# A chunked scan's software pipeline: four matrices made in two rounds, output parts in a kept bank, other rounds for most steps

## The reference, cut to what matters

```python
def wkv7_scan(state0, r, w, k, v, a_vec, b_vec, reverse):
    def step(S, inp):
        r_t, w_t, k_t, v_t, a_t, b_t = inp
        sa = jnp.einsum('bhij,bhj->bhi', S, a_t)
        S = (S * w_t[:, :, None, :] + sa[..., None] * b_t[:, :, None, :]
             + v_t[..., None] * k_t[:, :, None, :])
        return S, jnp.einsum('bhij,bhj->bhi', S, r_t)
    s_fin, ys = lax.scan(step, state0, xs, reverse=reverse)
```

## Time and profile before

| what | us |
|---|---|
| runs, median (lowest, highest) | 2563.83 (2563.2, 2566.87) |
| profiled execution, first to last instruction | 2557.6 |
| PE busy in it | 2362.5 |
| stretch of the scan, first to last triangular copy | 1429 to 1748 |

### The profile page before, as it was taken

One profiled execution on the slowest core, in us unless ns is written; L12 is line 12 of the kernel. 1 busy time (PEld: TensorE's weight loads), 2 busy tenths in 40 slices (PEclk: granted clock), 3 DMA queues, 4 the chain that ended last, 5 costly groups with the idle time before them and its releaser, 6 DMA issues.

```text
span 2557.6 us, 38789 instructions
## 1 busy us (share of the span) xinstructions
PE 2362.5 (92%) x15040; PEld 1754.2 (69%) x15040; DVE 1744.3 (68%) x3348; ACT 1052.7 (41%) x2064; POOL 338.9 (13%) x534
## 2 busy tenths in 40 slices
PE   7999999799989799899999899988999998998997
PEld 3788887464888699843454577776577765766775
DVE  4875787677756687723657666666678884748996
ACT  4222222224221434421144244433467783346884
POOL 0111110010001011000200233331012210001210
PEclk9999999899999999999998999999899999999998
DMA  8555654242326488511110000000379993115995
GB/s 302 198 201 193 221 196 157 89 149 80 109 73 216 148 279 277 201 50 58 36 39 33 34 3 3 2 2 2 106 255 352 337 323 112 71 58 204 343 336 203
DMA packets 115064, 386.98 MB, mean 151 GB/s; under 512 B 20161, under 2 KB 22337, under 8 KB 114625
## 3 DMA queue, kind: packets, MB, share of 16 engines
q1 hardware_dynamic: 76640, 276.33, 30.6%
q0 software_dynamic: 34848, 95.47, 10.9%
q10 hardware_dynamic: 3392, 12.70, 1.3%
HBM read 389.66 MB, written 26.21 MB: 163 GB/s over the span
## 4 chain that ended last, share of the span: by engine, by line
PE 36%; DVE 14%; DMA 7%; ACT 5%; issue 3%; POOL 0%; DVEq 0%; ACTq 0%; SPq 0%; POOLq 0%
PE ps L143 34%; DMA RG<-in_w 5%; DVE moe0wl L152 3%; PE ps L146 2%; DVE moe1wl L152 2%; DMA AR<-in_a 2%; DVE rwMM L172 1%; DVE f2wl L152 1%; DVE acc L160 1%; ACT moe0wh L149 1%; DVE H L160 1%; ACT moe1wh L149 1%; DVE rwXF L152 1%; ACT rwWU L149 1%; DVE rwXX L152 0%
## 5 line engine op out<-in xcount | busy, mean ns | idle before, releaser
L143 PE MATMUL ps<-H,RG 128*128 128x256 f32 (+2 forms) x1088 | 360.1, 487 | 14.0 <-ACT H L149 14.0
L160 DVE SCALAR_TENSOR_TENSOR acc<-AR,cs,acc 128x512 f32<-128x512 f32 x420 | 295.4, 746 | 43.3 <-DMA AR<-in_a 41.5
L143 PEld LDWEIGHTS ps<-H,RG 128*128 128x128 f32 (+1 forms) x1088 | 205.3, 192 | 151.3 <-issue 135.0
L152 DVE TENSOR_TENSOR moe0wl<-RG,moe0wh 128x1024 fp32r<-128x1024 f32 x144 | 173.7, 1220 | 39.1 <-ACT moe0wh L149 35.0
L149 ACT ACTIVATE moe0wh<-RG 128x1024 fp32r<-128x1024 f32 x144 | 151.1, 1061 | 69.9 <-DMA RG<-in_w 37.4
L199 POOL DMA_DIRECT2D AR<-in_a x152 | 82.2, 541 | 696.5 <-DVE acc L160 506.2
L149 ACT ACTIVATE f1wh<-RG 128x1024 fp32r<-128x1024 f32 x66 | 69.7, 1061 | 229.9 <-PE ps L143 229.8
L152 DVE TENSOR_TENSOR moe1wl<-RG,moe1wh 128x1024 fp32r<-128x1024 f32 x120 | 144.3, 1219 | 21.3 <-ACT moe1wh L149 17.8
L143 PE MATMUL ps<-f1hh,f1wh 128*128 128x512 f32 x352 | 142.7, 405 | 4.6 <-DVE f1hl L152 4.6
L149 ACT ACTIVATE moe1wh<-RG 128x1024 fp32r<-128x1024 f32 x120 | 126.1, 1060 | 44.0 <-DMA RG<-in_w 24.5
L143 PE MATMUL ps<-f1hh,f1wl 128*128 128x512 f32 x352 | 141.3, 401 | 0.0
(11 more groups left out here) (634 smaller groups left out, 5765.9 us busy)
## 6 DMA issues: line engine op xcount, KB each, us to landing
RG<-in_w SPq DMA_DIRECT2D x525, 512.0 KB, 4.7
AR<-in_a POOLq DMA_DIRECT2D x152, 512.0 KB, 3.7
moe0back<-moe_outs ACTq DMA_DIRECT2D x4, 1024.0 KB, 8.1
CT<-in_consts ACTq DMA_DIRECT2D x1, 2546.0 KB, 13.3
X<-in_x ACTq DMA_DIRECT2D x1, 2048.0 KB, 11.7
moe_rows<-moe0ht POOLq DMA_DIRECT2D x4, 512.0 KB, 4.9
moe1back<-moe_outs ACTq DMA_DIRECT2D x2, 1024.0 KB, 5.9
X<-in_ctx ACTq DMA_DIRECT2D x1, 1024.0 KB, 5.7
```

Source lines behind the costliest of these rows:

```text
L143: return Silent() if self.e is None else self.e.matmul(out, lhs, rhs, start=start, stop=stop, skip_group_check=True)
L152: return Silent() if self.e is None else self.e.tensor_tensor(out, a, b, op)
L160: return Silent() if self.e is None else self.e.scalar_tensor_tensor(out=out, in0=a, scalar=s, in1=b, op0=op0, op1=op1)
```

## The change

The rounds in which each step of a unit stands, before and after:

| step | engine | before | after |
|---|---|---|---|
| decays, first part / second part | ACT | 1 / 1 | 0 / 1 |
| clear MM | POOL | 1 | 0 |
| RA, KB q=0 / KB q=1, state scaled | DVE | 2 / 2 | 2 / 3 |
| matrices q=0 / q=1 | PE | 3 / 3 | 3 / 4 |
| masked copies q=0 / q=1 | DVE | 3 / 3 | 4 / 4 |
| MC | ACT | 3 | 4 |
| transpose of KB; its copy | PE; ACT | 3; 3 | 5; 5 |
| ML(i) | POOL | 3 + 2i | 4 for i = 0, else 4 + 2i |
| lev i; t i | PE; ACT | 5, else 4 + 2i | same |
| wu0 | PE | 16, behind lev 6 | 16, ahead of lev 6 |
| xx i, x i | PE, DVE | 5 + 2i | same |
| state x RA, KBt1 v | PE | 19 | 17 |
| u parts, v x MM | PE | 19 | 19 |
| state updated; y written | DVE | 19; 19, y first | 20; 21 (20 in the last 8 units) |

Each matrix now has a bank of its own (four banks of 256 columns in use in place of two of 512), so DVE makes four masked copies of 128x256 in place of two of 128x512. st and y share one bank, number 7, which is taken out of the turn for the scan (`turning = 7`). In each round a unit now has three slots, which are all run before the next unit's turn; they order steps within one unit only. The core of the diff:

```diff
+        to = self.clock()
+        yield from to(3, 2)
+        self.mm_pe(e, n, 0, KB, RA)
+        yield from to(4, 0)
+        self.mm_pe(e, n, 1, KB, RA)
...
+            if i == 6:
+                yield from to(r, 0)
+                self.wu0_pe(e, n, RA, MM, state, v)
...
-            if li == 0:
-                self.wu0_pe(e, n, RA, MM, state, v)
...
+            if i == 0:
+                yield from to(r, 2)
+                ps = g.banks.take(("kbt", n))
...
+        yield from to(17, 2)
+        out = g.banks.take(("y", n), 7)
...
+        e.matmul(out[:, 0:P], state, RA[:, P:2 * P], True, False)
+        if step < 3:
+            e.wait_ge(*S.act.at(("kbt", n)))
+            e.matmul(out[:, P:2 * P], KBt[:, 1, :], v, False, False)
...
+        yield from to(4, 2)
+        e.wait_ge(*S.dve.at(("mk", n, 0)))
         for b in (slice(0, 64), slice(64, 128)):
             e.activation(B["MC"][b, :, :], B["MM"][b, :, b], ACT.Copy).then_inc(*a.up(("mc", n)))
...
-                e.copy_predicated(two(MM[:, hh, :]), mask, two(g.banks.of(("mm", n, hh))[:, :])).then_inc(*v.up(("mk", n)))
+                e.copy_predicated(MM[:, hh, q * 256:(q + 1) * 256], mask,
+                                  g.banks.of(("mm", n, q, hh))[:, 0:256]).then_inc(*v.up(("mk", n, q)))
...
+        yield from to(4, 0)
+        masks(0)
+        yield from to(4, 2)
+        masks(1)
...
-            yield
+            yield from to(4 + 2 * i if i else 4, 1)
             if i:
-                yield
                 e.wait_ge(*S.pe.at(("t", n, i - 1)))
                 e.wait_ge(*S.dve.at(("x", n, 0)))
             else:
                 e.wait_ge(*S.act.at(("mc", n)))
```

More of the change, by code:

```diff
@@ L2652, in run @@
             for u in list(running):
-                if next(u, "over") == "over":
+                if "over" in [next(u, "over") for _ in range(self.SLOTS)]:
                     running.remove(u)
-            assert len(running) <= self.NS
             if close is not None and r in self.CLOSE:
@@ L2662, in run, with clock, to @@
                 beside(e, r)
+    def clock(self):
+        at = [0]
+        def to(r, slot):
+            for _ in range(r * self.SLOTS + slot - at[0]):
+                at[0] += 1
+                yield
+        return to
     def last(self, j):
@@ L2757, in unit_pe @@
         src, dst = self.halves(d)
-        yield
-        yield
[L2760 to L2778, removed]
-        for i, li in self.levels():
-            yield
+        to = self.clock()
[3 more added lines that the diff above has]
+        self.mm_pe(e, n, 1, KB, RA)
+        for i, li in self.levels():
+            r = 4 + 2 * i if i else 5
+            if i == 6:
+                yield from to(r, 0)
+                self.wu0_pe(e, n, RA, MM, state, v)
+            yield from to(r, 1)
             key = ("lev", n, i)
@@ L2884, in unit_act @@
         g.banks.done(("kbt", n), a.now())
[L2885 to L2898, removed]
+        for i, li in self.levels()[1:]:
+            yield from to(4 + 2 * i, 1)
+            e.wait_ge(*S.pe.at(("t", n, i)))
+            rows = slice(0, P) if li else dst
+            e.activation(T1[rows, :, :], two(g.banks.of(("lev", n, i))[rows, 0:128]), ACT.Copy).then_inc(*a.up(("t", n, i)))
+            g.banks.done(("lev", n, i), a.now())
+            if li == 0:
+                e.wait_ge(*S.pe.at(("wu0", n)))
+                e.activation(WU[:, 0, :], g.banks.of(("wu0", n))[:, 0:P], ACT.Copy).then_inc(*a.up(("wu0", n)))
+                g.banks.done(("wu0", n), a.now())
+        yield from to(18, 0)
         e.wait_ge(*S.pe.at(("wu1", n)))
@@ new lines, in unit_dve @@
+        yield from to(20, 0)
+        if step < 3:
+            last = e0 + (P - 1 if d == 0 else 0)
+            e.wait_ge(*S.pe.at(("st", n)))
+            e.wait_ge(*S.pe.at(("y", n)))
+            e.wait_ge(*v.at(("ts", n)))
+            for lo in (0, 64):
+                q = slice(lo, lo + 64)
+                e.tensor_tensor(state[q, q], state[q, q], g.banks.of(("y", n))[q, P + lo:P + lo + 64], ADD).then_inc(*v.up())
+            e.wait_ge(*v.now())
+            e.tensor_scalar(state, state, EB[:, last:last + 1], None, MUL).then_inc(*v.up())
+            v.note(("end", n))
+            yield from to(21, 0)
@@ L2967, in unit_dve @@
         g.banks.done(("y", n), v.now())
[L2968 to L2978, removed]
+        if step == 3:
+            v.note(("end", n))
     def unit_pool(self, e, n, step, d, j, B):
@@ L2982, in unit_pool @@
         MM, MC, ML = B["MM"], B["MC"], B["ML"]
-        yield
+        to = self.clock()
+        yield from to(0, 0)
         if n >= self.NS:
```

156 lines of the change are left out of this document (81 added, 75 removed).

## The result

The changed kernel takes 2631.6 us (median of 4 runs, 2627.6 to 2634.6) against 2565.4 for the kernel before in the same comparison: ratio 1.0251 [1.0231, 1.0271]. The profiled execution has a span of 2627.4 us against 2557.6, which is +69.8. (A run of the changed kernel and the profile of the same execution differ by 1.8 us, 2629.2 against 2627.4. So of the 6.2 us between span and median before, only about 1.8 lie around the instructions; the rest is the difference between executions.) The prediction said slower by 21 us, with a range that ended at 2605; the direction is right, the size is three times too small.

A forecast was written before the change was run, and what follows sets the result against it. PE was taken to bound the kernel, losing time to waits in its own list. 10.12 - 1.60 + 0.1 + 2.00 = 10.62 us a period gave +14, clock falls +7: 2585 us, range 2570 to 2605.

The forecast's parts named there:

- old waits go: On PE in the scan, four waits (xx 5, lev 6, lev 4, xx 4) vanish: 1.45 us, 1.60 with refills, a period.
- PE's own work in a period: On PE in the scan, 8.67 us of the old 10.12 us period was counted as its own work.
- chain xx 2 to lev 3: From xx 2 on PE through x 2, two masked copies, compaction, ML(0) and ML(3) to lev 3: 3.54 us.
- new wait at lev 3: On PE at lev 3, a wait for POOL in each period: 3.54 - 1.54 = 2.00 us.
- clean periods, in all: In the scan, 28 of 32 units counted at +0.50 us a period: +14 us.
- the clock, over the scan: In the scan, PE's granted clock falls after some gaps: 5 falls at 1.5 us, +7 us.
- far bound: Masked copy of 256 columns on DVE: 0.73 us if nothing is saved against 512 columns; 0.46 was taken.
- one such change costs PE little: On PE, the split matrices, each half followed by weights of another shape, cost perhaps 0.1 us a period.
- no cost: POOL's clearing of MM, some 0.9 us, stands ahead of ML(1), which PE needs only some 2 us after lev 3.
- one period in five or six: In the scan, how often the gap makes the clock fall: 5 falls at 1.5 us, +7 us.
- the clock did not hold: Rival that the clock holds in the scan: only the +14 us remain, 2578 us, or 2572 with cheap copies; chance 0.25.
- many falls: Rival in the scan: 14 clock falls at 1.5 us on the +14 give +35, 2599 us; chance 0.20 with long chain.

The follow-up runs named there:

- the run with all moves: Changed kernel with q=0 masked copies in round 3, ML(0) behind ML(3) on POOL, clearing in round 2, state update in round 19: 2551.1 us, ratio 0.9936.
- the run with the early transpose: Changed kernel with the transpose of KB in round 4, behind the second half of the matrices, instead of round 5: 2603.0 us, ratio 1.0142.
- the filled gap: Changed kernel plus one useless 512-column product on PE ahead of xx 5 in each unit: 2611.8 us, ratio 1.0155.
- the run with all four at once: Changed kernel with both halves of the matrices in round 3 on PE and both inputs in round 2: 2669.3 us, ratio 1.0392.
- the early copies: Changed kernel with the q=0 masked copies in round 3, ahead of x 2 of the older unit, instead of round 4: 2577.8 us, ratio 1.0015.
- the later clearing: Changed kernel with ML(0) behind ML(3) on POOL and the clearing of MM in round 2 instead of 0: 2587.5 us, ratio 1.0081.
- the clearing alone moved: Changed kernel with only POOL's clearing of MM moved, to round 2 from round 0: 2633.5 us, ratio 1.0267.

## Why the prediction was right in its direction and wrong in its size

| term | predicted | measured | from |
|---|---|---|---|
| old waits go | -1.60 | all four gone | timeline of PE |
| PE's own work in a period | 10.12 - 1.60 + 0.1 = 8.62 | 9.1 | changed kernel; the run with all moves |
| chain xx 2 to lev 3 | 3.54 | 3.59 | timelines |
| new wait at lev 3 | 2.00 | 1.87 (bracket 1.70) | timeline of PE |
| wait at lev 1 | 0 | 0.39 | timeline; the run with the early transpose |
| clean period | 10.62 | 11.40 | masked copies; the filled gap |
| clean periods, in all | +14 | +33 | first 26 periods |
| the clock, over the scan | +7 | +18 to 19 | first 26 periods; the filled gap |
| last five units | none | +6 | masked copies |
| ahead of the scan, closing, behind | none | +13 | the two traces |

The lower four lines are the whole: +21 predicted, +70 measured.

*Right.* PE's wait moved to lev 3, and it is POOL's list that holds it: with ML(0) behind ML(3) lev 3 doesn't wait, and with the copies ahead of x 2 nearly all of the loss is gone. The chain came out within 0.05 us, and the masked copy at 0.434, nearer to the 0.46 taken from the additions than to either bound. (The far bound of 0.73 would add 2 x 0.27 = 0.54 to a period and not 0.51; that changes nothing here.)

By the formula of the Trainium skill's page "VectorE: DVE Perf Modes", section "The TRN2 errata", the estimate was 0.39 us. The row says 0.434, so the formula was low again, by a tenth, as it was at 512 columns.

*Wrong, first: PE's own work, "one such change costs PE little".* I counted +0.1 for the changes of shape and took 0.15 off for refills behind the old waits, which no run shows: 8.62 us, where 9.1 was measured. The price was read from a group of eight products that takes 1.07 with its one change. But the change makes more of them than that one. Each half of the matrices takes 0.63 or 0.64 (1586.21 to 1586.85, 1588.70 to 1589.33), 1.27 in place of 1.07, and the run with all four at once has 1.07 again. The first transposed output product now stands alone between other shapes (1586.85 to 1587.27, 0.42). A group of four 64x64 products behind another shape takes 0.28 where one behind its like takes 0.24 (1589.33 to 1589.61; 1552.98 to 1553.22 in the earlier trace rows), and 0.33 to 0.36 where another shape follows it (1588.37 to 1588.70; lev 0, 1591.97 to 1592.33). So in these traces one change costs some 0.1 us ahead of it and 0.04 behind it. That changes of shape are the whole of the 0.4 to 0.5 is read from such distances; a run that takes them all away was not made.

*Wrong, second: behind lev 3 nothing was looked for.* I named the clearing and said "no cost", because ML(1) is needed 2 us later. The clearing indeed costs nothing there. But in the same list a step had moved that does feed lev 1: the transpose of KB, now two rounds later. The additions of x 0 on DVE wait for it, since they write over KB, and POOL's ML(1) waits for them. Lev 1 starts at 1582.78 where 1582.15 + 0.24 was possible:

```profile
1580.87 0.44 PE L146 MATMUL ps<-CT,rwa 128*128 128x128 f32 x2
...
1582.15 0.40 PE L143 MATMUL ps<-nv,rwXX 64*64 64x64 f32 x8
1582.78 0.35 PE L143 MATMUL ps<-rwa 64*64 64x64 f32 x5 [0.23 <-POOL rwa L152]
...
1581.41 0.29 DVE L152 TENSOR_TENSOR rwa<-rwa 128x128 f32<-128x128 f32 x1 [0.78 <-PE ps L146]
...
1582.18 0.45 POOL L152 TENSOR_TENSOR rwa<-rwa 128x128 f32<-128x128 f32 x1 [1.18 <-DVE rwa L152]
```

With the transpose early, that wait is gone; the run gives 0.26 of its 0.39 us back, the rest goes to the products of lev 1 and xx 6, whose instructions took turns in the changed kernel and now stand apart. With PE's own work from the run with all moves, the terms make 9.1 + 1.87 + 0.39 = 11.36 us; 11.40 was measured. Over 26 periods that is the +33, 19 us of the 49 that the forecast is short (69.8 - 21).

*Wrong, third: the number of falls.* I took "one period in five or six" and 1.5 us each. It was one in two at 1.1 us (one of them, the 15.44, at 4.1), 11 us of the 49. The rows of before held both outcomes, and my choice between them had no ground but that they were two. In the steady part the runs with a wait of 1.03 us or less at lev 3 or lev 0 had no fall (the early copies, the later clearing, the filled gap); with 1.34 at lev 3 there were seven in 23 periods, with 1.70 twelve (eleven with the clearing alone moved), with 2.35 eighteen. But the kernel with ML(0) behind ML(3) had three, of 10.2 us each, with 1.03 at lev 0 beside waits of 0.37 and 0.55, so the longest wait alone does not decide it.

The other 19 us, the last five units and what lies outside the masked copies, I had put at nothing, and their cause stays open.

The Trainium skill's page "TensorE: Matmul & The Clock Gate", section "Why this matters for your kernels", advises against idle gaps of PE between bursts of matmuls, and the length that it warns of is longer than any of these waits. The traces differ: with a gap of 1.7 us in each period of 11.5, the clock fell in every other one, and with the gap filled it did not.

The rivals: the clock did not hold; "many falls" was the nearest (2599), with 14 falls where there were 15, and it too lacked the 0.78 us a period. The far bound of the range was made from the copies' price alone, +28 at most, while the unknowns that mattered were PE's own work and the wait at lev 1.

## What to carry to other kernels

When steps move between products of different shape, count the changes of shape in the new order on PE, and price each by the distance between starts on both sides of one, not by the mean of a group. When a wait is expected, follow each moved step to the consumer behind it too, in every list; a wait that is taken away lets the next one show, and that one's price is in the same trace. And where PE is the bound and idles in each period, first look at the granted clock in short stretches: filling the gap with useless work won 1.0% here, and closing it won more. Two periods that alternate are compared as a pair: read one by one, the clearing seems to be worth 0.1 us here.

## What the runs showed of the hardware

- A scaling of 128x128 in SBUF on DVE took 1.12 us in place of 0.29 when POOL's clearing (0.95) started 0.09 behind it, and it ended 0.08 behind the clearing. With the early copies the same instruction took 0.464 (18 of them): it started at 1586.84, 0.56 behind the clearing's start, and ended 0.07 behind the clearing's end (1587.23). The Trainium skill's page "SBUF — State Buffer", section "SBUF: two separate sides", says that a VectorE instruction in a mode with two ports and a GpSimd one take a shared pair of ports as an exclusive lock, whichever starts first, so that the other blocks for the whole instruction. The ends just behind the clearing's agree; that the one with the earlier start wins does not show here, since in the first case the scaling's record begins first. Nor does either run show which mode the scaling is in.
- PE at 0.50 of the clock is slower by less than half: the period with a stretch of 3.4 us at 0.50 is 1.1 us longer, not 1.7. Of the difference, 0.39 is the wait at lev 1, which these periods don't have; the last 0.2 stays open.
- A product of no use took 1.1 us of PE and made the kernel 1.0% faster.
